# Three low parts of each mixer's input move to GpSimd, and the order around them changes

## The chip, the cores and the metric

The kernel runs on one core of a Trainium2 chip. The metric is device time in microseconds for one execution, here the median of three runs. Engines are named as in the profile: PE is TensorE (PEld its weight loads), DVE is VectorE, ACT is ScalarE, POOL is GpSimd, SP is SyncE, which here issues the weight loads.

## The reference

One inference step of a diffusion backbone: four layers, each with a SwiGLU feed-forward, a token mixer and a second feed-forward, each behind an RMS norm with shift, scale and gate from a condition. 128 context tokens and 256 latent tokens (384 in all), model width 1024, all in float32.

```python
for i in range(DEPTH):                                  # kind = A, B, C, D in turn
    xp = half_ffn(xp, ...); xs = half_ffn(xs, ...)
    hp = modulate(xp, norm_mix[i], mp[3], mp[4])        # rms_norm(x) * (1 + scale) + shift
    hs = modulate(xs, norm_mix[i], ms[3], ms[4])
    # A: windowed GQA with a sink logit; B: global GQA with rotary; C: latent attention; D: neighbourhood
    q, k, v = gqa_project(hs, w_qkv, q_norm, k_norm, heads, kv_heads)   # A, B, D: heads RMS-normed
    q, k = apply_rope(q, ang), apply_rope(k, ang)                        # A, B: latent tokens alone
    o = attention(q, k, v, cached keys, cached values)
    xs = xs + ms[5] * merge_heads(o, w_o)
    xp = half_ffn(xp, ...); xs = half_ffn(xs, ...)
```

## The kernel before

There are twelve stages `s`, three a layer; the middle one of each three is a mixer, of kind A, B, C or D (`stage_kind`). Activations lie with channels on the 128 partitions: `x` is 8 blocks (`KD`) of 128 channels by 384 tokens. Each product is made of three float32r products, hi x hi, hi x lo and lo x hi: every operand is rounded to a high part, and the low part is what the rounding left. ScalarE makes high parts, VectorE low parts. Weights come in chunks in two buffers; for each chunk ScalarE makes `w_hi` (`split_hi`, L1238) and VectorE `w_lo` (`split_lo`, L1566, a subtraction of two SBUF inputs over up to 3072 columns).

**The head of a mixer.** `mixer_stats` (L784, L787) sums squares with small matmuls, POOL takes the power -1/2 (`power`, L674), `broadcast` (L794) turns it over all partitions into a PSUM bank. Between these TensorE runs filler matmuls (`stay_busy`, L768) of 512 columns. VectorE's `norm` then goes over the 8 blocks k: `by_norm(k)` (L1658) scales x into `tmp[k % 2]`, in two parts, 128 context and 256 latent columns, with one input in PSUM; ScalarE's `modulated_hi` (L1268) adds the shift and rounds to `h_hi`; VectorE's `low(k)` (L1665) adds the shift again and subtracts `h_hi`, both inputs in SBUF, giving `h_lo`. `by_norm(k)` waits for `low(k - 2)`, whose `tmp` it overwrites. TensorE's `first_projection` (in C `compress`) runs over the blocks k, three token tiles of three matmuls each (L863, L1056); for tile 0 it waits for the context part of `low(k)`, for tile 1 for the latent part. After the eight blocks VectorE splits the stage's second weight chunk (`split_lo(CB[s], 1, ...)`), and makes the rotary tables times gains (`mixer_constants`, L1752, L1757; only A and B, and small ones in C). TensorE needs that chunk for `projection(s, 1, t)`, right after the first.

**Groups.** A and B have 4 groups g of 4 query heads and 1 key head, C and D 8 groups of 2. A projected group is copied from PSUM to `raw` by ScalarE (`raw`, L1312), squared (`squares_of`, L1329, into `nrm`), summed per head on VectorE (`head_sums`, L1779, L1782), the power is taken on POOL (`power`, L674, into `hrs`). In A and B POOL's `rotate` makes the crossed products of the rotation (L711, two of 320 columns) and the context's gain (L715), VectorE's `rotate_heads` finishes it (L1809, L1810), and `scale_heads` (L1832) scales the key only; queries are scaled in the exponential. POOL then issues the output DMAs of keys and values (L754, L755). On POOL everything stands in one queue: the power, the constants' loads (L687), then what the groups need; in D also the loads of the bias, 8 ahead of the groups.

**Batches.** Attention runs over 16 batches b, two for each pair of heads (`BATCHES`). For batch b the engines run, each in its own order, `scores` (L951 to L961) on TensorE, `maximum` (L1889 to L1913) on VectorE, the exponentials (L1364, L1376) on ScalarE, `inverse` (L1925 to L1931) on VectorE, which scales the probabilities, `turn_p` (L973) on TensorE two batches later, `p_copy` (L1393) on ScalarE, `values` (L1009, L1012) three batches later, and `o_hi` (L1399), `o_lo` (L1939) of its result. `turn_qk` (L923) turns the next pair's queries and keys, `qk_copies` (L1347, L1351) takes them out of PSUM. Between them TensorE runs parts of the group after next (`fills`, `projection`) and, at the end, of the output projection (`output`, L1037). For even b VectorE runs `inverse(b - 1)` ahead of `maximum(b)` (`early`), for odd b behind it. `proj_bank` gives each projected tile its PSUM bank; from group 2 on all tiles of A, B and D share bank `B_P`, so a tile waits for the copy of the one before (`n` in `projection`).

## Time and profile before

| | |
|---|---|
| median of 3 runs | 2948.01 us (2947.73 to 2948.53) |
| the profiled execution | 2948.41 us, its span 2946.5 us, mean granted TensorE clock 0.998 |
| PE busy | 2901.9 us, 98% |
| PEld busy | 2810.2 us, 95% |
| DVE busy | 2270.9 us, 77% |
| ACT busy | 1260.8 us, 43% |
| POOL busy | 167.0 us, 6% |
| DMA | 490 MB, 166 GB/s |

The page gives busy time by engine over the whole span. A stage is read with the view of windows, the order of work with the timeline of one engine, the cost of one operation with the groups by line. The mixers lie at about 316 to 478 (A), 1027 to 1179 (B), 1729 to 1920 (C) and 2470 to 2671 us (D); the rest is feed-forward.

### The profile page before, as it was taken

The page shows a single profiled execution, that of the slowest core. Times are in us where ns is not written, and L with a number is a line of the kernel's source. Part 1 is how long each engine was busy: PE and PEld are TensorE (multiplying, and loading weights), DVE is VectorE, ACT ScalarE, POOL GpSimd, SP SyncE. Part 2 cuts the span into 40 slices and gives each one's busy share as a digit, 9 for nine tenths or more (in the row PEclk, how much of TensorE's full clock was granted, in tenths as well). Part 3 has the DMA queues.
Part 4 walks back from the last instruction along what each step waited for, and adds up shares of the span by engine and source line. Part 5 has one row for each costly group of instructions (what it writes and reads, how often), then busy time and mean ns, then how long its engine had stood idle before and what let it go on. Part 6 is the DMA issues. An engine that isn't in the chain of part 4 may idle for free.

```text
span 2946.5 us, 44402 instructions
## 1 busy us (share of the span) xinstructions
PE 2901.9 (98%) x17591; PEld 2810.2 (95%) x17591; DVE 2270.9 (77%) x3471; ACT 1260.8 (43%) x2001; POOL 167.0 (6%) x167
## 2 busy tenths in 40 slices
PE   8999989999999999999999999999999999999999
PEld 6999879999999988999999997899999999889999
DVE  6889887888787777788888876778888887777653
ACT  3332464443333266443333248644333333564432
POOL 0000220000000030000000012000000001320000
PEclk9999999999999999999999999999999999999999
DMA  7555304555455511555555531255545555324332
GB/s 289 207 213 220 137 31 157 192 205 201 172 192 207 207 63 64 197 190 201 205 185 187 216 120 46 73 199 186 205 188 193 192 204 196 106 71 176 128 141 95
DMA packets 87722, 490.22 MB, mean 166 GB/s; under 512 B 11824, under 2 KB 13168, under 8 KB 51376
## 3 DMA queue, kind: packets, MB, share of 16 engines
q1 hardware_dynamic: 83696, 480.42, 44.1%
q0 software_dynamic: 3904, 8.24, 1.1%
q8 instruction: 68, 1.11, 0.2%
q14 instruction: 54, 0.44, 0.0%
HBM read 485.33 MB, written 3.29 MB: 166 GB/s over the span
## 4 chain that ended last, share of the span: by engine, by line
PE 56%; issue 38%; DVE 3%; ACT 2%; DMA 1%; POOL 1%; SPq 0%; DVEq 0%; POOLq 0%; ACTq 0%
PE ps L823 16%; PE ps L842 8%; PE ps L828 8%; PE ps L863 6%; PE ps L1037 5%; PE ps L846 4%; PE ps L807 1%; PE ps L973 1%; PE ps L1012 1%; PE ps L1111 1%; DMA boot<-in_mod_w 1%; PE ps L954 1%; PE ps L958 1%; PE ps L923 0%; PE ps L1056 0%
## 5 line engine op out<-in xcount | busy, mean ns | idle before, releaser
L823 PE MATMUL ps<-h_hi,w_hi 128*128 128x386 f32 x2688 | 908.2, 338 | 0.0
L823 PE MATMUL ps<-h_lo,w_hi 128*128 128x386 f32 x2688 | 893.4, 332 | 0.0
L1566 DVE TENSOR_TENSOR w_lo<-w_raw,w_hi 128x2048 fp32r<-128x2048 f32 (+3 forms) x282 | 706.3, 2504 | 32.6 <-ACT w_hi L1238 32.3
L1586 DVE CUSTOM_DVE_ANT_0 F_junk<-F_slab,cond,mod_b 128x1024 f32<-128x1024 f32 x544 | 706.5, 1299 | 13.1 <-DVE mod L1586 0.5
L1238 ACT ACTIVATE w_hi<-w_raw 128x2048 fp32r<-128x2048 f32 (+4 forms) x278 | 578.6, 2081 | 15.1 <-DMA w_raw<-in_ffn_dn 11.1
L823 PEld LDWEIGHTS ps<-h_lo,w_hi 128*128 128x128 f32 x2688 | 512.5, 191 | 0.0
L823 PEld LDWEIGHTS ps<-h_hi,w_hi 128*128 128x128 f32 x2688 | 503.1, 187 | 0.3 <-ACT w_hi L1238 0.3
L828 PE MATMUL ps<-h_hi,w_lo 128*128 128x386 f32 x2688 | 494.4, 335 | 0.0
L842 PE MATMUL ps<-F_act_hi,w_hi 128*128 128x384 f32 x1408 | 473.6, 336 | 0.0
L842 PE MATMUL ps<-F_act_lo,w_hi 128*128 128x384 f32 x1408 | 473.3, 336 | 0.0
L828 PEld LDWEIGHTS ps<-h_hi,w_lo 128*128 128x128 f32 x2688 | 469.0, 187 | 0.0
L1282 ACT ACTIVATE sq<-sq 128x128 f32<-128x128 f32 x176 | 70.8, 402 | 827.1 <-DVE sq L1698 827.1
L1698 DVE TENSOR_TENSOR sq<-ps,rbc 128x386 f32<-128x386 f32 x176 | 98.5, 560 | 254.3 <-PE ps L828 234.4
L1273 ACT ACTIVATE sq<-x 128x384 f32<-128x384 f32 x96 | 50.2, 523 | 570.7 <-DVE x L1691 570.7
L842 PEld LDWEIGHTS ps<-F_act_hi,w_hi 128*128 128x128 f32 x1408 | 264.4, 188 | 0.0
L842 PEld LDWEIGHTS ps<-F_act_lo,w_hi 128*128 128x128 f32 x1408 | 264.3, 188 | 0.0
L846 PE MATMUL ps<-F_act_hi,w_lo 128*128 128x384 f32 x1408 | 254.7, 336 | 0.0
L846 PEld LDWEIGHTS ps<-F_act_hi,w_lo 128*128 128x128 f32 x1408 | 245.2, 188 | 0.0
L1691 DVE SCALAR_TENSOR_TENSOR x<-ps,mod,x 128x128 f32<-128x128 f32 x192 | 71.0, 411 | 136.8 <-PE ps L846 132.1
L863 PE MATMUL ps<-w_hi,h_hi 128*128 128x384 f32 x384 | 134.4, 350 | 3.4 <-ACT D_raw L1312 1.2
L1704 DVE SCALAR_TENSOR_TENSOR tmp<-tmp,sq 128x128 f32<-128x128 f32 x352 | 130.9, 413 | 5.7 <-ACT sq L1283 5.7
L674 POOL TENSOR_TENSOR stats_of<-stats_of,neghalf 128x3 f32<-128x3 f32 x12 | 10.3, 858 | 2180.7 <-DVE stats_of L1627 2180.7
(366 smaller groups left out, 3470.5 us busy)
## 6 DMA issues: line engine op xcount, KB each, us to landing
w_raw<-in_ffn_gu SPq DMA_DIRECT2D x176, 1024.0 KB, 4.8
F_slab<-in_mod_w SPq DMA_DIRECT2D x272, 512.0 KB, 5.6
w_raw<-in_ffn_dn SPq DMA_DIRECT2D x64, 1408.0 KB, 6.4
w_raw<-in_d_w SPq DMA_DIRECT2D x8, 1536.0 KB, 6.7
boot<-in_mod_w SPq DMA_DIRECT2D x8, 1024.0 KB, 10.2
w_raw<-in_a_w SPq DMA_DIRECT2D x4, 1536.0 KB, 6.4
w_raw<-in_b_w SPq DMA_DIRECT2D x4, 1536.0 KB, 6.6
w_raw<-in_c_w SPq DMA_DIRECT2D x8, 544.0 KB, 3.6
```

Of the source, the lines that this page charges most:

```text
L823: pe.matmul(ps[:, 2 * par + u, 0:N_MOVE], w[0][:, k, u, :], h[:, k, :], start=(k == 0 and h is h_hi), stop=False)
L828: mm = pe.matmul(ps[:, 2 * par + u, 0:N_MOVE], w[1][:, k, u, :], h_hi[:, k, :], start=False, stop=(k == KD - 1))
L842: pe.matmul(ps[:, B_DN[par], 0:N_TOK], w_hi[par][:, k * P:(k + 1) * P], y[:, k * N_TOK:(k + 1) * N_TOK], start=(k == 0 and y is act_hi), s ...
L846: mm = pe.matmul(ps[:, B_DN[par], 0:N_TOK], w_lo[par][:, k * P:(k + 1) * P], act_hi[:, k * N_TOK:(k + 1) * N_TOK], start=False, stop=(k == ...
L863: mm = pe.matmul(ps[:, proj_bank(kind, g, t), 0:QKV_W], x1[:, k, t * P:(t + 1) * P], rh[x2][par][:, k * QKV_W:(k + 1) * QKV_W], start=(k = ...
L1037: mm = pe.matmul(ps[:, wo_bank(m), 0:N_TOK], (w_hi, w_lo)[lh][par][:, cols], o[rh], start=(p == 0 and i == 0), stop=(p == PAIRS - 1 and i ...
L1238: act.activation(w_hi[par][:, 0:w], w_raw[par][:, 0:w], ACT.Copy).then_inc(w_split_hi.sem, 1)
L1566: dve.tensor_tensor(w_lo[par][:, 0:w], w_raw[par][:, 0:w], w_hi[par][:, 0:w], ALU.subtract).then_inc(w_split_lo.sem, 1)
L1586: dve.tensor_tensor_reduce(out=junk[:], in0=w, in1=cond[:, c, :], scale=scale, scalar=mod_b[:, n:n + 1], op0=ALU.mult, op1=ALU.add, accum_ ...
L1691: ins = dve.scalar_tensor_tensor(out=xs, in0=ps[:, bank, i:j], scalar=gate, in1=xs, op0=ALU.mult, op1=ALU.add)
L1698: dve.tensor_tensor(sq[par][:], ps[:, 2 * par, 0:N_MOVE], rbc[:], ALU.mult).then_inc(a_ready.sem, 1)
L1704: ins = dve.scalar_tensor_tensor(out=tmp[par][:, a0:a1], in0=tmp[par][:, a0:a1], scalar=tmp[par][:, N_TOK + c:N_TOK + c + 1], in1=sq[par][ ...
```

## The change

In each mixer, `low(k)` of the blocks 3, 5 and 7 is made by POOL, as two instructions a part (an add of the shift, in place in `tmp`, and a subtraction), behind the loads of the constants; `low_made` gives the semaphore to wait for. VectorE makes `low(0)` ahead of `by_norm(1)`, and each further low right after its own scaling. `mixer_stats` gets a filler matmul of 256 columns between its two sums. In A and B the rotation runs on VectorE, from `raw` into `nrm`, and `scale_heads` scales all five heads of a group into `qn` and copies the key once more; the exponential's scale is a constant then, and `maximum` takes one operation less in A. ScalarE's squares of a group wait for the last group's `qn`. In A and B `maximum(b)` comes ahead of `inverse(b - 1)` for every b. Tile 1 of group 2 (A, B, D) and of group 3 (D) has bank `B_O`, and the waits in `projection` are one tile later there, and at C's (3, 0). D's copies of turned queries and keys come first at batch 1. In C and D `p_copy` of batch 11 is moved from batch 13 into batch 12, ahead of the latent exponentials. Names that only follow from this (counters, tile widths, removed semaphores) are left out of the diff.

```diff
+POOL_LOWS = (3, 5, 7)
...
+    if t == 1 and (g == 2 or kind == "D" and g == 3):
+        return B_O
...
+                    c.mark(s, 2 * (KD - len(POOL_LOWS)) if c is h_ready else 2 * KD)
...
-                    v["qn"] = part("qn", [P, TT, 2 * HD if kind in "AB" else 4 * HD])
+                    v["qn"] = part("qn", [P, TT, (HPG[kind] + 2) * HD])
...
-            if kind == "D":
-                return scale_of[kind]
-            h = 2 * (p % per_pair(kind)) + i
-            return head_scales(kind, p // per_pair(kind))[:, t, h:h + 1]
+            return head_scales(kind, p)[:, t, i:i + 1] if kind == "C" else scale_of[kind]
+
+        def low_made(s, k, c):
+
+
+            if k in POOL_LOWS:
+                return h_pool_ready.sem, h_pool_ready.after(s, 2 * POOL_LOWS.index(k) + c)
+            return h_ready.sem, h_ready.after(s, 2 * (k - sum(j < k for j in POOL_LOWS)) + c)
...
+
+                def low(k):
+
+
+                    h_hi, h_lo = input_of(s)
+                    m = mod[:, 3 * KD * (s % 3):3 * KD * (s % 3 + 1), :]
+                    for c, (i, j) in enumerate(((0, P), (P, N_TOK))):
+                        pool.wait_ge(h_hi_ready.sem, h_hi_ready.after(s, 2 * k + c))
+                        z = tmp[k % 2][:, i:j]
+                        chain.link(pool.tensor_scalar(z, z, m[:, k, c:c + 1], None, ALU.add))
+                        pool.tensor_tensor(h_lo[:, k, i:j], z, h_hi[:, k, i:j],
+                                           ALU.subtract).then_inc(h_pool_ready.sem, 1)
...
+
+                for k in POOL_LOWS:
+                    low(k)
...
-                def rotate(g):
...
-                    for e in range(2):
-                        pool.tensor_tensor(v["rope"].rearrange(pair, two=2)[:, :, :, e],
-                                           raw[:, 1:TT].rearrange(pair, two=2)[:, :, :, 1 - e],
-                                           v["sg"].rearrange(pair, two=2)[:, :, :, e], ALU.mult)
...
-                    pool.wait_ge(rsq_ready.sem, rsq_ready.after((s, g)))
-                    pool.tensor_tensor(raw[:, 0, :], raw[:, 0, :], v["g"][:], ALU.mult).then_inc(rope_ready.sem, 1)
...
-                    if kind in "AB":
-                        rotate(g)
...
+                pe.matmul(ps[:, B_WARM, 0:2 * P].rearrange("p (b c) -> p b c", b=2), ones[:],
+                          ident[:].unsqueeze(1).to_broadcast([P, 2, P]), start=True, stop=True)
                 pe.wait_ge(sq_ready.sem, sq_ready.after(s - 1, KD - 1))
                 for t in range(TT):
                     mm = pe.matmul(ps[:, t, 0:1], sq[1][:, t * P:(t + 1) * P], ones[:, 0:1], start=False, stop=True)
...
-                    pe.wait_ge(raw_ready.sem, n - 1 if kind == "C" and g == 2 and t else n)
+                    if (kind == "C" and (g == 2 and t or (g, t) == (3, 0))) or (kind == "D" and g < 4 and t):
+                        n -= 1
+                    elif kind != "C" and g == 2 and t:
+                        n -= 1
+                    pe.wait_ge(raw_ready.sem, n)
...
-                            pe.wait_ge(h_ready.sem, h_ready.after(s, 2 * k + t))
+                            pe.wait_ge(*low_made(s, k, t))
...
-                        at = (p % per_pair(kind)) * P if what == "q" else 0 if kind in "AB" else HPG[kind] * HD
-                        src = v["raw"][g % 4] if what == "q" and kind in "AB" else v["qn"]
+                        at = (p % per_pair(kind)) * P if what == "q" else HPG[kind] * HD
                         for t in range(TT):
-                            mm = pe.transpose(ps[:, bank, t * P:(t + 1) * P], src[:, t, at:at + P], ident[:])
+                            mm = pe.transpose(ps[:, bank, t * P:(t + 1) * P], v["qn"][:, t, at:at + P], ident[:])
...
-                if b == 0 and kind == "C":
-                    pe.wait_ge(raw_ready.sem, raw_ready.after((s, 2), proj_tiles(kind) - 1))
+                if b == 0:
+                    g_last, t_last = {"A": (2, 1), "B": (2, 1), "C": (2, 3), "D": (3, 1)}[kind]
+                    pe.wait_ge(raw_ready.sem, raw_ready.after((s, g_last), t_last))
...
-                        act.wait_ge(hms_ready.sem, hms_ready.after((s, g - 1)))
+                        done = hms_ready if kind == "D" else qn_ready
+                        act.wait_ge(done.sem, done.after((s, g - 1)))
...
-                    if 2 <= b < BATCHES + 2:
+                    if 2 <= b < BATCHES + 2 and not (per_pair(kind) == 1 and b == BATCHES - 3):
                         p_copy(s, b - 2)
...
-                    copies_first = kind in "AB" or not fills(kind, b) or (kind == "C" and b == 1)
+                    copies_first = kind in "AB" or not fills(kind, b) or (kind in "CD" and b == 1)
...
+                        if per_pair(kind) == 1 and b == BATCHES - 4:
+                            p_copy(s, b - 1)
                         latent_probabilities(s, b)
...
                 by_norm(0)
+                low(0)
                 by_norm(1)
+                low(1)
                 for k in range(2, KD):
-                    low(k - 2)
-                    dve.wait_ge(h_ready.sem, h_ready.after(s, 2 * k - 3))
+                    dve.wait_ge(*low_made(s, k - 2, 1))
                     by_norm(k)
-                low(KD - 2)
-                low(KD - 1)
+                    if k not in POOL_LOWS:
+                        low(k)
...
-                lat = v["raw"][g % 4][:, 1:TT, 0:(HPG[kind] + KVPG[kind]) * HD]
-                dve.wait_ge(rope_ready.sem, rope_ready.after((s, g)))
-                chain.link(dve.tensor_tensor(lat, lat, v["cg"][:], ALU.mult))
-                chain.link(dve.tensor_tensor(lat, lat, v["rope"][:], ALU.add))
+                nn = (HPG[kind] + KVPG[kind]) * HD
+                raw, z = v["raw"][g % 4][:, :, 0:nn], v["nrm"]
+                pair = "p t (e two) -> p t e two"
+                dve.tensor_tensor(z[:, 0, :], raw[:, 0, :], v["g"][:], ALU.mult)
+                for e in range(2):
+                    dve.tensor_tensor(v["rope"].rearrange(pair, two=2)[:, :, :, e],
+                                      raw[:, 1:TT].rearrange(pair, two=2)[:, :, :, 1 - e],
+                                      v["sg"].rearrange(pair, two=2)[:, :, :, e], ALU.mult)
+                chain.link(dve.tensor_tensor(z[:, 1:TT], raw[:, 1:TT], v["cg"][:], ALU.mult))
+                chain.link(dve.tensor_tensor(z[:, 1:TT], z[:, 1:TT], v["rope"][:], ALU.add))
...
-                if kind in "AB":
-                    key = v["raw"][g % 4][:, :, (nh - 1) * HD:nh * HD].unsqueeze(2).to_broadcast([P, TT, 2, HD])
-                    r = head_scales(kind, g)[:, :, nh - 1:nh].unsqueeze(3).to_broadcast([P, TT, 2, HD])
-                    dve.tensor_tensor(qn.rearrange("p t (c d) -> p t c d", c=2), key, r,
-                                      ALU.mult).then_inc(qn_ready.sem, 1)
-                    return
-                src = v["raw"][g % 4][:, :, 0:nh * HD]
+                src = v["raw"][g % 4][:, :, 0:nh * HD] if kind == "D" else v["nrm"][:]
                 r = v["hrs"][0][:, 0:TT * nh].rearrange("p (t h) -> p t h", h=nh).unsqueeze(3)
                 chain.link(dve.tensor_tensor(qn[:, :, 0:nh * HD].rearrange("p t (h d) -> p t h d", h=nh),
                                              src.rearrange("p t (h d) -> p t h d", h=nh),
                                              r.to_broadcast([P, TT, nh, HD]), ALU.mult))
-                cols = slice(HPG[kind] * HD, nh * HD)
-                dve.tensor_tensor(v["kout"][:], qn[:, 0, cols], v["g"][:, cols], ALU.mult).then_inc(qn_ready.sem, 1)
+                if kind == "D":
+                    cols = slice(HPG[kind] * HD, nh * HD)
+                    dve.tensor_tensor(v["kout"][:], qn[:, 0, cols], v["g"][:, cols], ALU.mult).then_inc(qn_ready.sem, 1)
+                else:
+                    dve.tensor_copy(qn[:, :, nh * HD:(nh + 1) * HD], qn[:, :, (nh - 1) * HD:nh * HD]
+                                    ).then_inc(qn_ready.sem, 1)
...
+                if kind == "C":
+                    scales = head_scales(kind, g)[:, 2 * x:2 + x]
+                    dve.scalar_tensor_tensor(out=nb.rearrange("p (a h) -> p a h", h=2),
+                                             in0=mx.rearrange("p (a h) -> p a h", h=2), scalar=-1.0, in1=scales,
+                                             op0=ALU.mult, op1=ALU.mult).then_inc(max_ready.sem, 1)
+                    return
+                if kind != "A":
                     dve.tensor_scalar(nb, mx, -scale_of[kind], None, ALU.mult).then_inc(max_ready.sem, 1)
                     return
 
...
-                ins = dve.scalar_tensor_tensor(out=nb2, in0=by_head(mx), scalar=-1.0, in1=scales,
-                                               op0=ALU.mult, op1=ALU.mult)
-                if kind != "A":
-                    ins.then_inc(max_ready.sem, 1)
-                    return
-                chain.link(ins)
-                dve.tensor_tensor(nb2, nb2, of_heads(v["nsink"]), ALU.min).then_inc(max_ready.sem, 1)
+                nb2 = nb.rearrange("p (a h) -> p a h", h=2)
+                dve.scalar_tensor_tensor(out=nb2, in0=mx.rearrange("p (a h) -> p a h", h=2), scalar=-scale_of[kind],
+                                         in1=of_heads(v["nsink"]), op0=ALU.mult, op1=ALU.min).then_inc(max_ready.sem, 1)
                 dve.wait_ge(max_ready.sem, max_ready.after((s, p, x)))
                 dve.tensor_tensor(st[:, 3, 0:n].rearrange("p (a h) -> p a h", h=2), nb2, of_heads(v["sink"]),
                                   ALU.add).then_inc(sink_shifted.sem, 1)
...
+                    early = kind in "CD" and b % 2 == 0
```

## Rows read from the trace of the kernel before

**Rows 1.** Windows A, B: length; busy PE, PEld, DVE, ACT, POOL; PEclk; DMA.
```profile
316.00:478.00 162.00, 148.91 (x1054) 132.17 (x1053) 127.45 (x265) 100.02 (x233) 37.10 (x32) 0.97 0.19 69
1027.00:1179.00 152.00, 146.06 (x1058) 129.45 (x1056) 111.05 (x199) 98.68 (x217) 35.32 (x30) 1.00 0.21 72
```

**Rows 2.** Waits of TensorE, whole span: us, times, longest.
```profile
PE ps L1009 <- DVE A_oT_lo L1939: 6.5, 5, 1.7
...
PE ps L923 <- ACT B_pt L1393: 3.9, 3, 1.5
PE ps L923 <- ACT A_pt L1393: 3.9, 3, 1.4
...
PE ps L1111 <- ACT C_kraw L1318: 1.2, 1, 1.2
PE ps L923 <- ACT D_pt L1393: 1.2, 1, 1.2
PE ps L863 <- ACT D_raw L1312: 1.2, 2, 0.6
PE ps L918 <- ACT C_pt L1393: 1.0, 1, 1.0
PE ps L787 <- ACT sq L1273: 1.0, 1, 1.0
...
PE ps L951 <- ACT D_kt L1351: 0.8, 1, 0.8
PE ps L863 <- ACT A_raw L1312: 0.8, 2, 0.6
PE ps L863 <- ACT B_raw L1312: 0.8, 2, 0.6
```

**Rows 3.** Timeline, VectorE, head of B: start, length, instruction.
```profile
1030.94 1.39 DVE L1658 SCALAR_TENSOR_TENSOR tmp<-x,mod,ps 128x128 f32<-128x128 f32 x4 [1.25 <-PE ps L794]
1032.24 0.74 DVE L1665 SCALAR_TENSOR_TENSOR h_lo<-tmp,mod,h_hi 128x128 fp32r<-128x128 f32 x2
...
1040.85 1.40 DVE L1665 SCALAR_TENSOR_TENSOR h_lo<-tmp,mod,h_hi 128x128 fp32r<-128x128 f32 x4
1042.16 3.35 DVE L1566 TENSOR_TENSOR w_lo<-w_raw,w_hi 128x3072 fp32r<-128x3072 f32 x1
```

**Rows 4.** Timeline, ScalarE, head of B.
```profile
1033.40 0.91 ACT L1268 ACTIVATE h_hi<-tmp,mod 128x128 fp32r<-128x128 f32 x2 [0.49 <-DVE tmp L1658]
```

**Rows 5.** Timeline, TensorE, head of B.
```profile
1030.64 1.88 PE L768 MATMUL ps<-ident,ones 128*128 128x512 f32 x4
1032.74 0.41 PE L863 MATMUL ps<-w_hi,h_hi 128*128 128x384 f32 x1 [0.21 <-DVE h_lo L1665]
```

**Rows 6.** Chain that ended last, head of A: start, length, line, count.
```profile
323.39 24.22 PE ps L863 x138
```

**Rows 7.** Timeline, GpSimd, first groups of B.
```profile
1050.07 4.06 POOL L715 TENSOR_TENSOR B_raw<-B_raw,B_g 128x320 f32<-128x320 f32 x1
...
1060.56 2.00 POOL L711 TENSOR_TENSOR B_rope<-B_raw,B_sg 128x320 f32<-128x320 f32 x2 [1.56 <-ACT B_raw L1312]
1062.53 0.87 POOL L715 TENSOR_TENSOR B_raw<-B_raw,B_g 128x320 f32<-128x320 f32 x1
```

**Rows 8.** Timeline, VectorE, first groups of B.
```profile
1050.06 3.35 DVE L1566 TENSOR_TENSOR w_lo<-w_raw,w_hi 128x3072 fp32r<-128x3072 f32 x1
...
1062.08 0.51 DVE L1905 SCALAR_TENSOR_TENSOR B_stat<-B_stat,B_hrs 128x4 f32<-128x4 f32 x1
```

**Rows 9.** Groups by line, VectorE: busy us, mean ns, idle.
```profile
L1779 DVE TENSOR_REDUCE B_hms<-B_nrm 128x15 f32<-128x960 f32 x4 | 4.6, 1144 | 0.1
...
L1911 DVE TENSOR_TENSOR A_stat<-A_stat,A_nsink 128x4 f32<-128x4 f32 x8 | 1.3, 162 | 0.3
```

**Rows 10.** Windows in A; PEclk is the granted clock.
```profile
319.40:322.90 3.50, 3.43 (x8) 1.89 (x8) 2.36 (x8) 2.24 (x5) 3.50 (x8) 0.51 0.93 361
...
408.20:415.00 6.80, 5.77 (x26) 4.87 (x27) 6.45 (x15) 2.78 (x10) 2.48 (x1) 0.50 0.00 0
```

37 lines of the change are left out of this document (10 added, 27 removed).

## The prediction

> **What bounds the kernel now.** I read the views in this order: busy shares, then TensorE's own waits, then the order of work at the head of one mixer, engine by engine. TensorE is busy in 98% of the span. In the mixer stages it stands still for 13.1 us in A and 5.9 us in B [rows 1], and the list of its waits says for whom [rows 2]; the matmuls of the feed-forward stages (L823 to L846) aren't in that list, and no edit touches those stages. All that can move lies in the four mixers. There TensorE waits for copies and low parts that ScalarE and VectorE make late. VectorE is no bound on average (127 of 162 us in A), but it is late at single points.
>
> The head of a mixer decides most here. VectorE scales block k (L1658), ScalarE rounds it (L1268), VectorE makes the low part (L1665), TensorE takes nine matmuls a block. Before, these are interleaved: after the first four scalings a pair of lows and a pair of scalings alternate, 1.43 us a block (1032.24 to 1040.85 is six blocks), and all of it is done at 1042.2 [rows 3]. TensorE starts at 1032.74 after 0.2 us of idling [rows 5] and never waits again in its 72 matmuls: 138 of them take 24.22 us [rows 6], so 0.176 us each, 1.58 us a block, 12.7 us in all. VectorE then splits the next weight chunk, 1042.16 to 1045.51 [rows 3], and TensorE ends its 72 at 1045.4. So the lows are hidden, with little slack, and the split ends level with TensorE. It is bad ground to add latency to.
>
> **Part 1, low parts of blocks 3, 5 and 7 on GpSimd.** Removed from VectorE: three pairs of L1665, 0.74 us each in the row [rows 3], some 2.2 us a mixer. Since they were hidden, that is worth nothing by itself. Added: four GpSimd instructions a block (an add and a subtract for 128 columns, the same for 256), each waiting for the one before.
> - Subtract, two inputs: the trace has 320 columns at 0.87 us [rows 7]. In proportion 256 columns are 0.70 and 128 are 0.35; with a fixed part more, I take 0.73 and 0.45.
> - Add of a per-partition scalar, one input: no row. It is at most a subtract, and hardly under half of one. I take 0.35 and 0.50, nearer the top, since the nearest row is the two-input one [rows 7].
> - Three hand-offs of 0.14 by estimate: no row shows GpSimd waiting for itself, so 0.05 to 0.2. Sum 1.18 + 0.85 + 0.42 = 2.45 us a block, 2.1 to 2.8. TensorE eats a block in 1.58.
>
> The rule of the Trainium skill that speaks against this part is in its page "GPSIMD Engine Reference", section "Engine selection": elementwise work belongs on VectorE, GpSimd being about twice as slow with two inputs and roughly at line rate with one. By that last clause the adds would be nearer 0.25 and 0.36 and each head some 0.6 us cheaper; no row here shows it.
>
> **The port.** While VectorE ran a split (1050.06, 3.35 us [rows 8]), a GpSimd multiply of 320 columns issued at 1050.07 took 4.06 us instead of 0.87 [rows 7]: it ended 0.73 after the split. The other way round, VectorE's tiny L1905 took 0.51 us at 1062.08 [rows 8] and ended as GpSimd's L711 did [rows 7], where such an operation needs 0.16 [rows 9]. So GpSimd and a VectorE instruction with two SBUF inputs shut each other out. L1665 and the split (L1566) are of that kind; L1658, with one input in PSUM, isn't. The Trainium skill says the same, page "SBUF — State Buffer", section "SBUF: two separate sides": the shared port pair is an exclusive lock held for the whole instruction. By that rule this change is slower; without it it would not be (rival 1).
>
> **The head of B, timed from the first scaling (1030.94).** The new order does scale, wait for the rounding (a pair takes 0.91 us on ScalarE [rows 4]), low, one block after the other: 1.72 us a block for 0, 1 and 2, against 1.43 before. Block 0's low is ready 0.5 us sooner, but TensorE's filler matmuls (L768) end only at 1032.52 [rows 5], so that gain is 0.2 to 0.3. Then:
> - block 3: rounded at 5.9 and 6.4, GpSimd ends its halves at 7.0 and 8.5; TensorE comes at 6.4 and waits 0.7 + 1.0 us;
> - block 5: scaling 5 needs GpSimd's block 3 (same buffer), so it starts at 8.6; TensorE waits 0 to 0.3;
> - block 7: scaling 7 needs block 5 and starts at 12.0. VectorE goes straight on to the split at 12.7, before ScalarE has rounded block 7 (12.8). GpSimd is shut out until 16.0, and ends the halves at 16.9 and 18.7. TensorE comes at 14.7 and waits 2.4 + 1.3 us.
> TensorE ends the 72 at 19.9 instead of 14.6: +5.3 us. With the cheap and the dear add and subtract: +4.2 and +6.3. A is alike: +5.3. In C the split has 2304 columns instead of 3072, so 0.8 us less of shutting out, and little else on VectorE: +4.3. D has no gain tables to make beside block 7: +4.7. Sum 19.6 us (15.4 to 23.6). VectorE's split and tables end before TensorE in every case, so nothing more is behind it. GpSimd's own queue: the constants' loads are issued before the lows; D's bias loads (eight) and the first power stand behind block 7 and slip, but the first score that needs them slips as well.
>
> **The clock.** In A TensorE ran at a granted 0.51 from 319.4 to 322.9 and at 0.50 from 408.2 to 415.0 [rows 10], each after idle gaps of 1 us or more (the first after the 1.0 us wait at L787 [rows 2]). The 256-column filler put into that gap costs nothing (the gap hides it) and, if it keeps the clock at its upper level, A's four fillers after the broadcast take B's 1.88 us [rows 5] instead of nearly twice that; of these 1.5 us the low part, ready sooner, lets 0.9 count (estimate). But block 7 now brings 3.7 us of idling with three matmuls in it, longer than either of those gaps. Each 3.4 us at the half level loses some 1.7 us. I count about three of four heads: +5 us (0 to 14).
>
> **Part 2, rotation of A and B on VectorE.** GpSimd's three multiplies go (and with them its blocking of VectorE); VectorE gets one of 320 columns, two strided of 320, a scaling of 960 instead of 384 columns and a 192-column copy. A reduction of 960 columns takes 1.14 us [rows 9], so 320 are some 0.45 and 576 more some 0.6; with the copy 0.45 + 2 x 0.45 + 0.6 + 0.2 = 2.1 us a group, 17 us in both stages. For groups 1 to 3 TensorE's projections hide most of it. For group 0 it stands before the first transposes: there GpSimd's blocked multiply no longer holds up L1809, so the net is +0.3 in B, +0.5 in A.
>
> **Part 3, order of the batches.** In A and B an even batch's maximum now comes before the last batch's scaling, so its exponentials and the copies behind them start about 1.1 us sooner; in A one small operation (0.16 [rows 9]) of each maximum is merged away. The waits this can shorten: L923 for A_pt and B_pt, 3.9 us each, and L1009 for A_oT_lo, 6.5 us [rows 2], with A's second half-clock stretch hanging on them. The longer rotation eats the gain at the batches where it falls. I take A -4.4, B -1.5 (together -10 to +1).
>
> **Part 4, banks and copies.** A second tile in its own bank removes waits for raw copies: 0.8 in A, 0.8 in B, 1.2 in D, 1.2 in C [rows 2], and with restarts I take -1.0, -1.0, -1.4 and, ScalarE in C being busy, only -0.8. D's copies first at batch 1: 0.8 [rows 2], -0.9. The early copy at batch 12: 1.0 in C, 1.2 in D [rows 2], -1.0 and -1.2, though the exponentials behind it then wait for TensorE. Sum -7.3 (-9 to -3).
>
> **Sum.** Heads +19.6, filler in A -0.9, clock +5.0, rotation +0.8, order -5.9, banks and copies -7.3: +11.3 us. The profiled execution took 2948.4 us (span 2946.5), 0.4 above the median of 2948.0, so 2959.5 us.
>
> **Rivals.** Rival 1, faster: the port doesn't bar a one-input add, or GpSimd gets in ahead of the split, so block 7 is made in time. Then a head costs about +1.3 us and only from GpSimd's slowness; 5.2 - 0.9 + 0.8 - 13.2 = -8: 2940 us. For it: one-input GpSimd work is in no row. Against: GpSimd's 4.06 us beside a split [rows 7]. 0.12. Rival 2, no change: the heads are cheap (15.4), the clock holds, and parts 3 and 4 take most of the waits (-18) [rows 2]: -3, 2945 us. For it: half of A's waits are of one kind. Against: VectorE has 2.1 us a group more to do. 0.20. Rival 3, clearly slower: dear adds (23.6), 10 us of half clock, gains of 8: +25, 2973 us. 0.10. The forecast's own case, 2951 to 2969: 0.58. A mechanism on the slower side that decides it is the split ahead of block 7: it turns the sum at the point where GpSimd's block 7 isn't done when TensorE comes, 14.7 us after the first scaling.
>
> **Chances.** 0.2% (6 us) is about what a measurement of this kernel tells from no change. Faster 0.14 (rival 1 and the edge of rival 2), same 0.22 (the rest of rival 2 and the edge of the forecast), slower 0.64. The range reaches from inside rival 2 to rival 3: 2943 to 2974.
>
> **What would show it.** Right: in each mixer's profile GpSimd's first instruction of block 7 at 3 us or more, beside L1566; TensorE waiting for h_lo of GpSimd 3 to 4 us at block 7 and 1.5 at block 3; a clock record at 0.5 behind it; the waits for raw copies in A, B and D gone. Wrong: 72 matmuls in 12.7 us at the head, or VectorE's split waiting instead of GpSimd; or A and B losing time at L923 because of the rotation.

## The result, and the profile after

The changed kernel takes 2967.24 us (2966.35 to 2968.20), the kernel before 2947.99 in the same runs: ratio 1.0065, 95% interval 1.0051 to 1.0079. It is slower by 19.2 us. The forecast was 2959.5 us with a range of 2943 to 2974: direction and range held, the size was short by 7.7 us.

The profiled execution took 2968.20 us, its span is 2966.4 (before 2946.5), its mean granted clock 0.996 (0.998). TensorE's busy time rose by 10 of these 20 us: a matmul at the lower clock, or the first one behind a wait, counts as busy for longer. The page of the changed kernel, busy time:

```profile
PE 2912.2 (98%) x17599; PEld 2815.6 (95%) x17599; DVE 2277.8 (77%) x3463; ACT 1251.4 (42%) x2001; POOL 179.2 (6%) x191
```

The line numbers shown are 3 to 12 higher than before: L868 was L863 (`first_projection`), L1065 was L1056 (`compress`), L931 was L923 (`turn_qk`), L981 was L973 (`turn_p`), L1018 was L1009 (`values`). TensorE's waits, whole span:

```profile
PE ps L868 <- POOL h_lo L697: 16.0, 15, 2.6
PE ps L981 <- DVE A_p L1942: 5.5, 3, 3.5
...
PE ps L1065 <- POOL h_lo L697: 4.2, 5, 1.4
...
PE ps L981 <- DVE B_p L1942: 1.7, 1, 1.7
PE ps L1120 <- ACT C_kraw L1327: 1.2, 1, 1.2
...
PE ps L931 <- ACT B_pt L1402: 1.0, 2, 0.6
```

The first and third are new: 20.2 us of waiting for low parts that GpSimd makes. The waits for raw copies in A, B and D, for A_oT_lo (6.5) and most of those for A_pt and B_pt [rows 2] are gone. In their place TensorE waits 5.5 and 1.7 us for the scaled probabilities of A and B, and 1.2 us for D_oT_lo.

The clock was at its lower level in five stretches of the mixers, four of them in or right behind a head (windows: length, then busy times; the granted clock is the 0.50 or 0.51 ahead of the last two numbers):

```profile
341.50:344.90 3.40, 3.40 (x12) 3.40 (x12) 0.61 (x1) 2.70 (x4) 0.00 (x0) 0.50 0.33 141
420.00:423.40 3.40, 3.21 (x22) 2.72 (x22) 3.30 (x7) 1.72 (x6) 1.11 (x2) 0.50 0.01 2
1051.50:1058.30 6.80, 5.64 (x19) 5.61 (x19) 1.71 (x4) 4.24 (x5) 1.27 (x3) 0.50 0.44 188
1758.10:1761.50 3.40, 3.35 (x12) 3.35 (x13) 0.00 (x0) 0.99 (x4) 0.00 (x0) 0.51 0.07 29
2505.60:2512.40 6.80, 6.28 (x20) 5.77 (x20) 1.31 (x2) 3.93 (x5) 6.63 (x11) 0.50 0.93 291
```

Before there were two such stretches, both in A [rows 10].

**The head of B, after.** GpSimd (start, length, instruction):

```profile
1038.51 0.61 POOL L696 TENSOR_SCALAR tmp<-tmp,mod 128x128 f32<-128x128 f32 x1 [4.08 <-ACT h_hi L1277]
1039.21 0.45 POOL L697 TENSOR_TENSOR h_lo<-tmp,h_hi 128x128 fp32r<-128x128 f32 x1
1039.64 0.96 POOL L696 TENSOR_SCALAR tmp<-tmp,mod 128x256 f32<-128x256 f32 x1
1040.68 0.72 POOL L697 TENSOR_TENSOR h_lo<-tmp,h_hi 128x256 fp32r<-128x256 f32 x1
...
1046.13 3.91 POOL L696 TENSOR_SCALAR tmp<-tmp,mod 128x128 f32<-128x128 f32 x1 [0.92 <-ACT h_hi L1277]
...
1050.67 1.16 POOL L696 TENSOR_SCALAR tmp<-tmp,mod 128x256 f32<-128x256 f32 x1
```

VectorE in the same head:

```profile
1041.44 1.39 DVE L1669 SCALAR_TENSOR_TENSOR tmp<-x,mod,ps 128x128 f32<-128x128 f32 x4 [1.01 <-POOL h_lo L697]
...
1045.25 0.74 DVE L1669 SCALAR_TENSOR_TENSOR tmp<-x,mod,ps 128x128 f32<-128x128 f32 x2 [1.01 <-POOL h_lo L697]
1045.90 3.35 DVE L1577 TENSOR_TENSOR w_lo<-w_raw,w_hi 128x3072 fp32r<-128x3072 f32 x1
1049.17 0.48 DVE L1764 TENSOR_TENSOR B_cg<-B_g,B_cos 128x320 f32<-128x320 f32 x1
```

And TensorE, at blocks 3 and 7:

```profile
1038.76 0.33 PE L868 MATMUL ps<-w_hi,h_lo 128*128 128x384 f32 x1
1039.71 0.45 PE L868 MATMUL ps<-w_hi,h_hi 128*128 128x384 f32 x1 [0.62 <-POOL h_lo L697]
1040.00 0.34 PE L868 MATMUL ps<-w_lo,h_hi 128*128 128x384 f32 x1
...
1050.74 0.44 PE L868 MATMUL ps<-w_hi,h_hi 128*128 128x384 f32 x1 [2.58 <-POOL h_lo L697]
...
1052.69 0.69 PE L868 MATMUL ps<-w_hi,h_hi 128*128 128x384 f32 x1 [1.16 <-POOL h_lo L697]
1053.17 0.52 PE L868 MATMUL ps<-w_lo,h_hi 128*128 128x384 f32 x1
```

The split began at 1045.90, GpSimd's first add of block 7 at 1046.13, and it took 3.91 us where the same add at block 3 took 0.61: it ended 0.79 after the split. TensorE waited 2.58 and then 1.16 us. Two details matter for the sum. The first is what a wait costs. A wait of 0.62 us put 0.95 us between the starts of two matmuls that otherwise lie 0.17 or 0.18 apart, 0.16 more than the wait itself. The profile counts idle time only from the end of the matmul before, 0.33 us behind its start, and its successor could have started 0.175 behind it: that is the 0.16. The next start is 0.29 behind instead of 0.18. So a wait costs 0.27 us beyond its idle time, and the other waits of these heads at the full clock show the same two gaps. The second is the lower clock: from 1053.17 on the starts lie 0.32 apart, so a matmul loses 0.145 us.

Where the 20 us are is read from two lengths per mixer, taken from the timelines. The head runs from the first sum of squares to 0.17 us behind the start of the last of TensorE's 72 matmuls; the mixer from GpSimd's power at its head to its next such power, in the feed-forward behind it. Microseconds, A, B, C, D; the kernels are those of the next section, the medians those of their timed runs.

```
                     median   head                    mixer
before               2948.0   20.1 17.9 17.9 17.9     160.2 150.3 190.9 199.6
changed              2967.2   26.1 25.8 24.4 25.2     160.9 156.0 197.2 205.2
e1_dve_lows          2946.1   19.4 18.7 18.7 18.7     154.3 150.9 192.7 199.4
e2_two_blocks        2948.4   21.5 20.8 20.8 20.8     156.9 150.2 193.2 200.2
e3_split_held        2959.3   22.2 21.7 21.7 21.4     159.7 152.3 195.2 203.8
e4_old_order         2936.7   18.9 18.2 18.2 18.2     153.2 147.3 190.7 197.0
e5_early             2941.3   18.9 18.2 18.2 18.2     157.4 148.6 190.8 197.0
e6_part1_alone       2977.7   26.3 25.5 23.3 24.6     167.6 159.2 196.3 207.1
e7_no_filler         2935.7   19.9 17.9 17.9 17.9     153.9 147.3 190.7 197.0
e8_part4_alone       2943.4   19.9 17.9 17.9 17.9     159.6 148.9 190.4 197.0
e9_rotation_alone    2947.0   19.7 17.9 17.9 17.9     158.4 150.0 191.3 199.6
e10_first_a          2937.8   18.9 17.9 17.9 17.9     154.8 149.4 190.7 197.0
e11_constant_add     2963.4   25.5 24.3 23.9 24.7     160.9 154.0 196.6 204.9
e12_filler_a         2935.5   18.9 17.9 17.9 17.9     153.0 147.3 190.7 197.0
```

The changed kernel's heads are 27.7 us longer in all (6.0 + 7.9 + 6.5 + 7.3), and behind the heads it is some 8 us shorter. The feed-forward stages differ by 0.3 us each at most.

### The profile page after: what moved, and what is told of

The parts are those of the page before. It is cut to its first block, busy times and chain, and to the rows that moved or that the text cites. A ratio compares the mean times of both kernels' runs of the same rounds, so it can differ in the third digit from the quotient of the medians.

```text
span 2966.4 us, 44428 instructions
## 1 busy us (share of the span) xinstructions
PE 2912.2 (98%) x17599; PEld 2815.6 (95%) x17599; DVE 2277.8 (77%) x3463; ACT 1251.4 (42%) x2001; POOL 179.2 (6%) x191
## 4 chain that ended last, share of the span: by engine, by line
PE 55%; issue 37%; DVE 3%; POOL 2%; ACT 2%; DMA 1%; SPq 0%; DVEq 0%; POOLq 0%; ACTq 0%
PE ps L828 16%; PE ps L847 8%; PE ps L833 8%; PE ps L868 6%; PE ps L1046 4%; PE ps L851 4%; PE ps L812 1%; PE ps L981 1%; PE ps L1021 1%; PE ps L1120 1%; POOL tmp L696 1%; DMA boot<-in_mod_w 1%; PE ps L962 1%; ACT h_hi L1277 1%; PE ps L966 1%
## 5 line engine op out<-in xcount | busy, mean ns | idle before, releaser
L1247 ACT ACTIVATE w_hi<-w_raw 128x2048 fp32r<-128x2048 f32 (+4 forms) x278 | 578.6, 2081 | 16.7 <-DMA w_raw<-in_ffn_dn 12.8
L868 PE MATMUL ps<-w_hi,h_hi 128*128 128x384 f32 x384 | 139.0, 362 | 16.0 <-POOL h_lo L697 16.0
```

Of the source, the lines that this page charges most:

```text
L868: mm = pe.matmul(ps[:, proj_bank(kind, g, t), 0:QKV_W], x1[:, k, t * P:(t + 1) * P], rh[x2][par][:, k * QKV_W:(k + 1) * QKV_W], start=(k = ...
L1247: act.activation(w_hi[par][:, 0:w], w_raw[par][:, 0:w], ACT.Copy).then_inc(w_split_hi.sem, 1)
```

## The experiments

The theory after the trace: part 1 loses some 30 us, by GpSimd's pace, by the split that shuts it out at block 7 and by the clock that falls behind it; the other parts gain some 11 us. Rivals: the loss is in GpSimd's slowness alone and not in the split; or it is in the batches, where VectorE now has the rotation.

### e1_dve_lows and e4_old_order: part 1 taken out

```diff
-POOL_LOWS = (3, 5, 7)
+POOL_LOWS = ()
```

e4_old_order has besides the head's order of before:

```diff
                 by_norm(0)
-                low(0)
                 by_norm(1)
-                low(1)
                 for k in range(2, KD):
+                    low(k - 2)
                     dve.wait_ge(*low_made(s, k - 2, 1))
                     by_norm(k)
-                    if k not in POOL_LOWS:
-                        low(k)
+                low(KD - 2)
+                low(KD - 1)
```

> The changed kernel with no low part on GpSimd (POOL_LOWS empty); the order scale, round, low and everything else stay. Theory (GpSimd's pace of 2.9 us a block and the split that shuts it out at block 7 make the heads 27.6 us longer, with some 9 us of half clock in and behind them): VectorE alone makes a block in 1.72 us (1032.48, 1034.20, 1035.92 in B), so the last low part comes some 1.0 us after TensorE wants it, and the split of the next chunk ends some 2.3 us after TensorE's 72 matmuls. A head is then about 20.5 us instead of 25.4, and the half clock behind block 7 shrinks to what a 2 us wait brings: 2944 us (2940 to 2950). GpSimd does no add or subtract, TensorE's waits for h_lo of GpSimd (20.2 us) are gone, a wait for w_lo takes their place. Rival 1 (the batch order and the rotation lose the time, GpSimd is hidden): 2965 us or more. Rival 2 (the new order costs VectorE nothing that TensorE sees): 2936 us.

> As e1_dve_lows (no low part on GpSimd), and VectorE's order in the head as before the change: scale 0, scale 1, then low(k - 2), scale k. Parts 2 to 4 and the filler stay. Theory: the head is that of before, 1.43 us a block, no wait at all, the split done when TensorE is; only parts 2 to 4 and the filler are left, worth 12 us of waits and 4 us of clock in A less 0.9 us for the filler in B, C and D: 2936 us (2932 to 2940), faster than both kernels. Rival (new order as good as the old): the same time as e1_dve_lows.

Measured: 2946.05 us (2945.34 to 2947.00; ratio to before 0.9994, 0.9984 to 1.0003) and 2936.69 us (2936.30 to 2937.59; 0.9962, 0.9947 to 0.9976). So part 1 costs 30.5 us on top of the others, and without it the rest of the change gains 11.2. The rivals "in the batches" and "order is free" fall. The new order alone costs 9.4 us, though no low part is on GpSimd. In e1_dve_lows VectorE's split begins at 1038.98 in B and TensorE's next matmul, the first that needs that chunk, waits for it:

```profile
1038.98 3.35 DVE L1577 TENSOR_TENSOR w_lo<-w_raw,w_hi 128x3072 fp32r<-128x3072 f32 x1
```

```profile
1042.47 0.42 PE L868 MATMUL ps<-w_hi,h_hi 128*128 128x384 f32 x1 [2.04 <-DVE w_lo L1577]
```

The head itself is only 0.5 us longer; the wait for `w_lo` stands behind it, in each mixer (6.1 us in A, B and D together, 1.2 in C). By the new order VectorE makes a block in 1.72 us instead of 1.43, so the split starts 13.7 us after the first scaling instead of 11.2 as before [rows 3], where it had ended level with TensorE.

### e2_two_blocks: block 7 back on VectorE

```diff
-POOL_LOWS = (3, 5, 7)
+POOL_LOWS = (3, 5)
```

> The changed kernel with POOL_LOWS = (3, 5): block 7's low part back on VectorE. Theory: the waits at blocks 3 and 5 stay (some 2.0 us a head), block 7's 3.7 us go, and a wait of about 1 us for the split, which now stands behind low(7), comes: 2.7 us a head less and some 5 us less of half clock, 2951 us (2946 to 2956). Rival 1 (the loss is in GpSimd's pace alone, spread evenly over three blocks): a third of the heads' 27.6 us goes, 2958 us. Rival 2 (batch order): no change, 2967 us.

Measured: 2948.43 us (2948.19 to 2948.88; ratio 1.0001, 0.9992 to 1.0011). Taken out in this sequence, block 7 costs 18.8 us of the 30.5, blocks 3 and 5 together 2.4, the order 9.4. An even spread over the blocks is out. The shares hold for this sequence only: blocks 3 and 5 stop TensorE for 7.9 us here, and most of that stands where e1_dve_lows waits 7.3 us for `w_lo`. No run has the three blocks on GpSimd in the order of before, so what GpSimd costs without the new order isn't shown. The waits are as expected:

```profile
PE ps L868 <- POOL h_lo L697: 5.9, 9, 1.0
...
PE ps L868 <- DVE w_lo L1577: 2.2, 3, 0.7
PE ps L1065 <- POOL h_lo L697: 2.0, 3, 0.9
```

The time is 2.6 us below what was expected; no half-clock stretch is left in or behind any head, where the expectation had kept some.

### e3_split_held: the split waits for GpSimd

```diff
                 norm(s)
+                dve.wait_ge(*low_made(s, KD - 1, 1))
                 split_lo(CB[s], 1, width(s, 1))
```

> The changed kernel with one wait more: VectorE begins the split of the second chunk only when GpSimd has made block 7's low part. All three blocks stay on GpSimd. Theory (an operation of GpSimd is shut out while VectorE runs an operation with two inputs in SBUF): GpSimd's first add of block 7 takes 0.6 us instead of 3.9, block 7 is made in 2.9 us, TensorE waits about 1 us for it instead of 3.7, but then some 2 us for w_lo, since the split ends 3.1 us later. The head gets 1 to 2 us shorter: 2961 us (2956 to 2965). Rival (the 3.9 us are GpSimd's own, from the wait or the pointer operand, not from the split): the add stays at 3.9 us, the split comes 3 us later on top, and the time rises by some 12 us to 2979 us.

Measured: 2959.31 us (2958.97 to 2959.46; ratio 1.0038, 1.0024 to 1.0052), 7.9 us below the changed kernel. GpSimd at block 7 of B, then VectorE, then TensorE:

```profile
1044.32 0.60 POOL L696 TENSOR_SCALAR tmp<-tmp,mod 128x128 f32<-128x128 f32 x1 [0.92 <-ACT h_hi L1277]
...
1045.44 0.92 POOL L696 TENSOR_SCALAR tmp<-tmp,mod 128x256 f32<-128x256 f32 x1
1046.45 0.73 POOL L697 TENSOR_TENSOR h_lo<-tmp,h_hi 128x256 fp32r<-128x256 f32 x1
```

```profile
1047.21 3.36 DVE L1577 TENSOR_TENSOR w_lo<-w_raw,w_hi 128x3072 fp32r<-128x3072 f32 x1 [3.04 <-POOL h_lo L697]
```

```profile
1050.72 0.41 PE L868 MATMUL ps<-w_hi,h_hi 128*128 128x384 f32 x1 [1.90 <-DVE w_lo L1577]
```

The add takes 0.60 us again: the 3.91 us were the split's doing, and the rival falls. Block 7 is made in 2.86 us, and TensorE does not wait for it in this head, where its clock had fallen for 3.4 us after block 3; in A and D, at the full clock, it waits 0.35 us. VectorE idles 3.04 us, and the debt is paid at `w_lo` (6.2 us in A, B and D, 1.1 in C). So neither of the two orders tried has both VectorE's split and GpSimd's block in time.

### e6_part1_alone: part 1 on the kernel before

The new tuple, `low_made`, POOL's `low` and the new order of `norm`, as in the change's diff, on the kernel before; nothing else.

> The kernel before with part 1 alone: the three low parts on GpSimd and the new order of the head; no filler, rotation, batch order and banks as before. Theory (the loss is the heads' and adds to the rest): what part 1 costs on top of the other parts is 2967.2 - 2936.7 = 30.5 us, so 2948.1 + 30.5 = 2978.6 us (2975 to 2983), with TensorE waiting some 20 us for h_lo of GpSimd. Rival (part 1 costs so much only with the filler's later scaling and the busier VectorE of the other parts): 2970 us or less.

Measured: 2977.66 us (2977.12 to 2979.72; ratio 1.0103, 1.0087 to 1.0118): +29.6 us over before, against +30.5 on top of the other parts. Within a microsecond part 1 adds to them; the rival falls.

### e11_constant_add: the add without its pointer

This kernel leaves the shift out of the low parts of blocks 3, 5 and 7, so its results are false; it serves for the time alone.

```diff
-                        chain.link(pool.tensor_scalar(z, z, m[:, k, c:c + 1], None, ALU.add))
+                        chain.link(pool.tensor_scalar(z, z, 0.0, None, ALU.add))
```

> The changed kernel with a constant 0.0 in place of the per-partition shift in GpSimd's add (the low parts of blocks 3, 5 and 7 so lack the shift); the instructions and waits are the same. If the pointer to the scalar is what makes the add dearer than the subtract (0.61 and 0.96 us for 128 and 256 columns against 0.45 and 0.72), the add falls to 0.35 and 0.5 us, a block to 2.2 us, the waits at blocks 3 and 5 by 0.7 us each and the one at block 7 by 0.6: 2961 us (2958 to 2964). If GpSimd's one-input operation is as dear with a constant: the same durations, 2967 us.

Measured: 2963.41 us (2961.91 to 2964.73), 3.8 below the changed kernel. Block 3 of B:

```profile
1037.80 0.54 POOL L696 TENSOR_SCALAR tmp<-tmp 128x128 f32<-128x128 f32 x1 [4.06 <-ACT h_hi L1277]
...
1038.83 0.89 POOL L696 TENSOR_SCALAR tmp<-tmp 128x256 f32<-128x256 f32 x1
```

0.54 and 0.89 us instead of 0.61 and 0.96: the pointer is 0.07 us of each. A one-input add in place is dearer on GpSimd than the two-input subtract (0.46 and 0.72) even with a constant. Neither expectation was right: these durations hardly moved, the time did. TensorE's waits for GpSimd fell from 20.2 to 17.3 us. Most of it is block 7, where the add beside the split took 3.52 us instead of 3.91 (last section).

### e5_early: part 3 undone

On e4_old_order:

```diff
-                    early = kind in "CD" and b % 2 == 0
+                    early = b % 2 == 0
```

> As e4_old_order, with part 3 undone: in A and B an even batch's probabilities are scaled ahead of its maximum again. By the prediction's term (-5.9 us, A -4.4 and B -1.5) the time rises from 2936.7 to 2942.6 us, and TensorE's waits for A_oT_lo (6.5 us) and for A_pt and B_pt (3.9 each) come back, while the waits for A_p (5.5) and B_p (1.7) go. The A mixer, from its power to the next one, goes from 153.2 back to 157.5 us, B from 147.3 to 148.8. Rival (the new waits for A_p eat what the order gives, and the gain in A comes from elsewhere): 2937 us.

Measured: 2941.33 us (2941.14 to 2942.30; ratio to before 0.9978, 0.9968 to 0.9987), so the order is worth 4.6 us by the medians, A 4.2 and B 1.3 by the mixers' lengths of the profiled executions, which lie 5.2 apart. The waits that come back are smaller than those of before, the ones for A_p don't all go. Part of A's gain is the clock: in e5_early it was at 0.50 for 3.4 us from 394.4 and for 6.8 from 414.9, in e4_old_order for one stretch of 3.4.

```profile
PE ps L1018 <- DVE A_oT_lo L1949: 4.2, 3, 1.9
PE ps L931 <- ACT B_pt L1402: 2.8, 3, 1.2
PE ps L931 <- ACT A_pt L1402: 2.8, 4, 1.0
...
PE ps L981 <- DVE A_p L1941: 1.5, 2, 1.1
```

### e7_no_filler: the filler taken out

On e4_old_order, the matmul of 256 columns in `mixer_stats` left out.

```diff
-                pe.matmul(ps[:, B_WARM, 0:2 * P].rearrange("p (b c) -> p b c", b=2), ones[:],
-                          ident[:].unsqueeze(1).to_broadcast([P, 2, P]), start=True, stop=True)
```

> As e4_old_order, without the 256-column filler between the two sums. By the prediction (0.9 us gained in A, nothing in B, C and D) the time rises by 0.9 to 2937.6 us. By the trace of the changed kernel the filler lengthens the way from the first sum to the power by 0.3 us in B, C and D, so A's gain, with the fall of the clock that comes back there, is about cancelled: 2936.7 us within 0.5.

Measured: 2935.67 us (2935.47 to 2937.71). The filler costs 1.0 us by the medians, 0.3 by the two profiled spans, and the two kernels' times overlap. In A it does what the prediction said: the head is 1.0 us shorter with it, and the stretch of 3.4 us at 0.50 that e7_no_filler has at 318.0 isn't there. In B, C and D it is in series. TensorE at the head of B without it, and in the changed kernel with it:

```profile
1021.45 0.72 PE L787 MATMUL ps<-ones,ssq 128*128 128x1 f32 x6
1022.15 0.83 PE L790 MATMUL ps<-ones,sq 128*128 128x1 f32 x6
```

```profile
1028.80 0.72 PE L787 MATMUL ps<-ones,ssq 128*128 128x1 f32 x6
1029.39 0.68 PE L788 MATMUL ps<-ident,ones 128*128 128x256 f32 x2
1029.90 0.72 PE L792 MATMUL ps<-ones,sq 128*128 128x1 f32 x6
```

The second sum starts 0.70 us behind the first without it and 1.10 with it; at the head's end 0.3 us of that is left.

### e8_part4_alone: banks and copies on the kernel before

The change's lines in `proj_bank` and `projection`, the first wait in `values`, D's `copies_first` and the early `p_copy`, on the kernel before.

> The kernel before with part 4 alone (banks, the waits in the projection, D's copies at batch 1, the early copy of batch 11). By the prediction -7.3 us (A -1.0, B -1.0, C -1.8, D -3.5): 2940.7 us. By the mixer lengths of e4_old_order, where C is only 0.2 us and D 2.6 us shorter than before: -4.8 us, 2943.2 us.

Measured: 2943.39 us (2942.31 to 2944.01; ratio 0.9984, 0.9974 to 0.9993), -4.7 us: A -0.6, B -1.4, C -0.6, D -2.6 by the mixers. In A the 0.8 us for raw copies are gone, but TensorE waits longer some batches later, where it was 6.5 and 3.9 before [rows 2]. That is 3.0 us more; against it stands the clock, which had been at its lower level there for 6.8 us [rows 10] and now stays up (1.00, third from the end):

```profile
PE ps L1016 <- DVE A_oT_lo L1948: 8.6, 6, 1.8
PE ps L929 <- ACT A_pt L1400: 4.8, 4, 1.4
```

```profile
408.20:415.00 6.80, 5.85 (x53) 4.86 (x54) 6.45 (x15) 4.21 (x11) 2.34 (x1) 1.00 0.01 2
```

In C the wait for C_kraw, 1.2 us [rows 2], is still there, here and in the changed kernel (L1120 above). In D the waits for D_pt, D_raw and D_kt, 3.2 us [rows 2], are gone, and the one for D_oT_lo grows from 0.3 to 1.2.

### e9_rotation_alone: part 2 on the kernel before

The changed kernel with parts 1, 3, 4 and the filler undone as above, so that the rotation on VectorE is left.

> The kernel before with part 2 alone: the rotation of A and B on VectorE, the heads scaled into qn, the constant scale in the exponentials and the merged maximum of A. By the prediction +0.8 us: 2948.8 us, C and D as before. If the 17 us more of VectorE show in the batches (the rotation stands ahead of maxima and scalings that TensorE waits for), 2952 us or more, with longer waits for A_oT_lo, A_pt and B_pt than 6.5, 3.9 and 3.9 us. If GpSimd was in the way before (its multiply held up the rotation by 4.06 us beside a split), 2946 us.

Measured: 2946.95 us (2944.88 to 2948.47; ratio 0.9996, 0.9986 to 1.0005): -1.2 us, which can't be told from no change. The waits for A_oT_lo fall from 6.5 to 4.0 and those for A_pt and B_pt from 3.9 to 2.7 and 2.8; new are 1.4 for A_p and 1.2 for B_oT_lo:

```profile
PE ps L1009 <- DVE A_oT_lo L1938: 4.0, 3, 1.9
```

So 2.4 us a group more on VectorE (0.48 three times, 0.6 more for the scaling, 0.3 for the copy) is not dearer than what GpSimd's share cost.

### e10_first_a and e12_filler_a: a better version

Both are e4_old_order with the filler in A alone (`if stage_kind(s) == "A":` ahead of it). e10_first_a has besides:

```diff
-                    early = kind in "CD" and b % 2 == 0
+                    early = b % 2 == 0 and (kind in "CD" or b == 10)
```

> As e4_old_order, with the filler in A alone, and at batch 10 of A and B the last batch's scaling ahead of the maximum again. In A TensorE waits 3.5 us for A_p there, since VectorE runs the rotation (2.9 us, 413.68 to 416.56 in the changed kernel) and then the maximum of the next batch (2.2 us) ahead of the scaling that TensorE needs; in B 1.7 us. Theory: the 2.2 us of the maximum leave the path: 2 us less in A with the fall of the clock there (1.5 us), 1 us less in B, and 0.3 to 0.9 us for the filler: 2932 us (2930 to 2934). Rival (the exponentials of batch 10 come 1.3 us later and TensorE waits for them instead): 2936 us.

> As e4_old_order, with the 256-column filler in A alone (batch order of the change, no early scaling). In e4_old_order the filler made A's head 1.0 us shorter than in e7_no_filler (18.9 against 19.9 us), and B's, C's and D's 0.3 us longer each (18.2 against 17.9). So A keeps its gain and the others lose nothing: 0.9 us below e4_old_order and 1.0 below e7_no_filler, 2935 us (2934 to 2936.5), some 13 us below the kernel before. Rival (A's filler is worth nothing over the whole mixer, since the clock falls later instead): the time of e7_no_filler, 2935.7 us.

Measured: 2937.77 us (2935.66 to 2939.54) and 2935.53 us (2934.68 to 2936.00; ratio 0.9957, 0.9943 to 0.9970). The first came out near its rival's time, not its own. Its 3.5 us wait for A_p is cut to 1.34, but two others follow at once, the second one of 1.06 us for A_pt:

```profile
409.89 0.87 PE L982 MATMUL ps<-ident,A_p 128*128 128x128 f32 x6 [1.34 <-DVE A_p L1942]
412.64 0.44 PE L1019 MATMUL ps<-A_pt,A_raw 128*64 128x128 f32 x4 [1.87 <-DVE A_oT_lo L1950]
```

I read this as VectorE having more work there than a batch lasts, so that the order only chooses who waits; no run tests it. The clock has a part in it too: this trace is of the slowest of five runs, with 6.8 us at 0.50 in A and 3.4 in B at 1117.3, while the two fastest (2935.66 and 2935.97 us) had a mean clock of 1.000. The second kernel has the lowest median of this study, 12.8 us below before and 31.7 below the changed one. Its distance to e7_no_filler (0.1 us) can't be measured, so its expectation and its rival aren't told apart.

## Why the prediction was right in direction and short in size

**Heads and clock: forecast +19.6 and +5.0, measured together +30.5 (29.6 alone).** This is the step that was mis-sized.

- The waits are what the head's timing gave. In B, block 3: 0.7 + 1.0 forecast, 0.62 + 0.94 measured; block 5: 0 to 0.3 against 0.39; block 7: 2.4 + 1.3 against 2.58 + 1.16. TensorE waited 20.2 us for GpSimd, the sum had 19.6.
- The price of stopping was left out: I took idle time as lost time. Each of the 20 waits costs some 0.27 us beyond its idle time, 5.4 us in all. Short holds at blocks 1 and 2, which the profile doesn't count as idle, cost 1 us more, and 1.9 come back because the 72 matmuls begin 0.5 us sooner in each head. Measured, the heads are 27.9 us longer than in e4_old_order. Some 3 of these are the lower clock within them, so 24.9 stand against the 19.6 of the sum.
- GpSimd's add was taken at 0.35 and 0.50 us and took 0.61 and 0.96, while its hand-offs were taken at 0.14 and took 0.09, nothing and 0.08. A block took 2.89 us instead of 2.45. It did not lengthen the waits much, because TensorE itself came later: 15.5 us after the first scaling, not 14.7, at block 7.
- The clock was counted as three of four heads by 1.7 us. It fell in four of four, and twice for 6.8 us: 59 matmuls start in those windows, which at 0.145 us each is some 8.5 us (an estimate: six of them have fewer columns). 24.9 and 8.5 are 33.4, so some 3 us must be given back behind the head; that ScalarE and VectorE had run ahead there is my reading. No run takes the clock out by itself.
- The mechanism holds: the split shuts GpSimd out at block 7 (e3_split_held), and block 7 is 18.8 of the 30.5 us (e2_two_blocks). What the text had as a part of GpSimd's slowness, the order of scale, round and low, is worth 9.4 us by itself (e1_dve_lows), since it makes the split late. In the changed kernel that wait for `w_lo` isn't there, because TensorE stands at block 7 meanwhile. The text timed the order at 1.72 us a block and never asked for the split without GpSimd.

**Filler: -0.9 forecast, +0.3 to +1.0 measured.** "The gap hides it" was read from A, the only head with a gap [rows 2]. In B, C and D the squares were ready and it stands in series, 0.3 us each.

**Rotation: +0.8 forecast, -1.2 measured**, not told from nothing. The work on VectorE was sized right (2.1 a group, 2.4 measured), the net for group 0 and the waits that shrink with it (A_oT_lo, A_pt, B_pt) were not.

**Order of the batches: -5.9 forecast, -4.6 measured** (A -4.4 against -4.2, B -1.5 against -1.3). Direction and reason were right, with the half-clock stretch of A as part of it; but the text looked for the rotation's price at L923 and it appeared at `turn_p`. In A TensorE waits 3.5 us until 420.19, because VectorE runs the last rotation (to 416.56) and a maximum before it scales the probabilities.

**Banks and copies: -7.3 forecast, -4.7 measured.** D was forecast at -3.5 and gave -2.6, 0.9 of it coming back as a wait for D_oT_lo; B -1.0 and gave -1.4. A (-1.0) gave -0.6, its waits for A_oT_lo and A_pt growing while its clock stayed up; C (-1.8) gave -0.6, its wait for C_kraw never touched by the edit.

The misses add up: part 1 is 5.9 us over, filler 1.2 to 1.9, order 1.3, banks 2.6, rotation 2.0 under; the parts together did 1.1 to 1.8 us better than one by one. No large error was hidden by another: all but the rotation's have one sign. Of the signs named ahead, the waits at block 3 and a clock record behind block 7 came in every mixer, and the waits for raw copies vanished in A, B and D. GpSimd's first instruction of block 7 took 3.9 us in A and B and 3.6 in D, but 2.8 in C, under the 3 us named, and TensorE waited 3.7 us at block 7 in A and B, but 2.3 in C and 2.7 in D. The text had VectorE and GpSimd shut each other out alike; that holds in part (last section). Rival 1 fell with the 3.91 us and e3_split_held, rival 2 with the clock, which fell in all four heads. Rival 3's costs (23.6 for the heads, 10 for the clock) were nearer the measured ones (24.9, 8.5) than the forecast's own; its sum came out too high because the other parts gained 11.2 us, not 8.

## What to carry to other kernels

When a helper engine gets a share of a chain, ask first what VectorE will start once it is relieved: here it was the weight split, 3.35 us long, which shut out GpSimd and made the share late. A step that ends level with the bounding engine has no slack, so its start must be timed too when only the order ahead of it changes. And price a wait of an engine whose instructions overlap as more than the idle time that the profile lists, here 0.27 us more each, plus what the clock does behind it.
